# Another order in the attention loop: scaling ahead of the fourth row of logits, exponentials behind the copies, silu one step earlier

## What is computed

```python
for i in range(DEPTH):                                   # DEPTH = 2
    x = x + 0.5 * swiglu(rms_norm(x, ffn1_norm[i]), ...)  # width 2816
    x = x + hybrid_mixer(rms_norm(x, mix_norm[i]), ...)
    x = x + 0.5 * swiglu(rms_norm(x, ffn2_norm[i]), ...)
    gate = sigmoid(rms_norm(x, ple_norm[i]) @ ple_w_gate[i])
    x = x + gate * rms_norm(p[i] @ ple_w_proj[i], ple_post_norm[i])
```

```python
s = einsum('bqhmd,bkhmd->bhmqk', qblk, k) * scale + bias
p = softmax(where(dist >= 0, s, NEG))
o_h = rms_norm(o_h, hgrn_out_norm) * silu(hg)
mixed = concatenate([o_nsa, o_d, o_h]); return mixed @ w_out
```

## Time and profile before

| | us |
|---|---|
| median of 3 runs | 2317.85 |
| lowest, highest | 2317.26, 2318.3 |
| profiled execution | 2319.65 |
| its span | 2317.8 |
| TensorE busy in the span | 2247.7 |
| VectorE, ScalarE, GpSimd busy | 1191.1, 899.1, 155.7 |

### The profile page before, as it was taken

How to read it: one execution, slowest core, us unless ns; L and a number is a source line. 1 busy time by engine, 2 the same in 40 slices (tenths; PEclk the granted TensorE clock), 3 DMA queues, 4 the chain that set the end, 5 groups by cost and what they waited for, 6 DMA issues and landing times. The chain is left out here.

```text
span 2317.8 us, 28783 instructions
## 1 busy us (share of the span) xinstructions
PE 2247.7 (97%) x11400; PEld 1777.9 (77%) x11400; DVE 1191.1 (51%) x1965; ACT 899.1 (39%) x1479; POOL 155.7 (7%) x155
## 2 busy tenths in 40 slices
PE   8999999998989999999999999999989999999998
PEld 6888887776657888888778888877766578888887
DVE  5444434575676444433664443345666754444336
ACT  5222223544664323223552232234556543222334
POOL 0000000043112000000000000001331110000000
PEclk9999999999999999999999999999999899999999
DMA  5333334322103233333223333343120123333332
GB/s 190 129 95 99 93 100 145 103 65 66 52 21 90 93 100 92 97 108 98 90 92 100 97 93 98 95 144 106 55 80 28 29 84 100 100 101 97 97 99 81
DMA packets 68991, 214.38 MB, mean 92 GB/s; under 512 B 8143, under 2 KB 15311, under 8 KB 68858
## 3 DMA queue, kind: packets, MB, share of 16 engines
q1 hardware_dynamic: 59344, 189.27, 26.5%
q10 hardware_dynamic: 9514, 23.27, 3.0%
HBM read 208.30 MB, written 5.40 MB: 92 GB/s over the span
## 5 line engine op out<-in xcount | busy, mean ns | idle before, releaser
L525 PE MATMUL main<-xh,wh 128*128 128x512 f32 x1896 | 757.0, 399 | 12.2 <-DVE xl L1474 8.0
L526 PE MATMUL main<-xl,wh 128*128 128x512 f32 x1896 | 741.2, 391 | 0.0
L527 PE MATMUL main<-xh,wl 128*128 128x512 f32 x1896 | 740.8, 391 | 0.0
L1467 DVE TENSOR_TENSOR wl<-raw,wh 128x1024 fp32r<-128x1024 f32 (+2 forms) x338 | 407.2, 1205 | 376.8 <-ACT wh L983 375.7
L983 ACT ACTIVATE wh<-raw 128x1024 fp32r<-128x1024 f32 (+3 forms) x372 | 377.8, 1017 | 479.8 <-PE main L527 451.6
L525 PEld LDWEIGHTS main<-xh,wh 128*128 128x128 f32 x1896 | 357.2, 188 | 113.9 <-issue 21.3
L527 PEld LDWEIGHTS main<-xh,wl 128*128 128x128 f32 x1896 | 357.5, 189 | 75.7
L526 PEld LDWEIGHTS main<-xl,wh 128*128 128x128 f32 x1896 | 357.5, 189 | 75.1 <-issue 4.3
L525 PE MATMUL main<-ffh,wh 128*128 128x512 f32 x704 | 273.9, 389 | 0.0
L526 PE MATMUL main<-ffl,wh 128*128 128x512 f32 x704 | 273.9, 389 | 0.0
L527 PE MATMUL main<-ffh,wl 128*128 128x512 f32 x704 | 273.9, 389 | 0.0
(11 more groups left out here) (244 smaller groups left out, 2087.5 us busy)
## 6 DMA issues: line engine op xcount, KB each, us to landing
raw<-in_ffn_gate SPq DMA_DIRECT2D x88, 512.0 KB, 3.6
raw<-in_ffn_up SPq DMA_DIRECT2D x88, 512.0 KB, 3.5
raw<-in_ffn_down SPq DMA_DIRECT2D x64, 448.0 KB, 3.3
raw<-in_w_in_t SPq DMA_DIRECT2D x40, 512.0 KB, 3.6
raw<-in_ffn_down SPq DMA_DIRECT2D x32, 512.0 KB, 3.5
raw<-in_wout SPq DMA_DIRECT2D x24, 384.0 KB, 3.2
w<-in_cmp_w ACTq DMA_DIRECT2D x16, 512.0 KB, 3.9
raw<-in_ple_gate SPq DMA_DIRECT2D x16, 512.0 KB, 3.3
```

The lines of the kernel that those rows point to most:

```text
L525: nc.tensor.matmul(out, lh, rh, start=start, stop=False, **kw)
L526: nc.tensor.matmul(out, lh, rl, start=False, stop=False, **kw)
L527: return nc.tensor.matmul(out, ll, rh, start=False, stop=stop, **kw)
L1467: nc.vector.tensor_tensor(wl[:, c % SLOTS, 0:n], raw[:, c % SLOTS, 0:n], wh[:, c % SLOTS, 0:n], ALU.subtract).then_inc(*tick("weights_lo", ...
```

## The change

Three things, in both layers:

- VectorE does rows one to three of `logits(u)`, then `scale(u-1)`, then row four of `logits(u)`.
- ScalarE does rows one to three of the exponentials of map u, then `head_factor` and `split`, then `turned(u-1)`, then row four of the exponentials. `turned(u-1)` now stands ahead of the silu and of `mixed_hi`, which stood ahead of it.
- The silu of the gates moves from step 5 to step 4, behind the fourth exponentials. The wait for the product of `dq1` stays in step 5, ahead of `mixed_hi`.

```diff
+                def exponentials(u, rows):
+                    for i in rows:
+                        for g in range(2):
+                            act.wait_ge(*done("logits", u, g, i))
+                            k = 8 * (u % 2) + 4 * g + i
+                            pr = probs[u % 2][g][:, row0(i):row0(i + 1)]
+                            nc.scalar.activation(pr, pr, ACT.Exp, bias=sm("nm", k), scale=-1.0,
+                                                 accum_out=sm("sum", k)).then_inc(*tick("probs", u, g, i))
...
                         if u < MAPS:
-                            for i in range(QT):
...
+                            exponentials(u, (0, 1, 2))
                         if u == 0:
                             head_factor(("hgrn", 2), HEAD)
...
                             split(CHUNK[("wout_early", OUT_AT[u][0])] + AHEAD)
-                        if u == 5:
+                        if u:
+                            turned(u - 1, ACT_TURNS[u - 1 < NSA_HEADS])
+                        if u < MAPS:
+                            exponentials(u, (3,))
+                        if u == 4:
 
                             act.wait_ge(*done("scaled", "hg2"))
                             nc.scalar.activation(z[:], z[:], ACT.Silu).then_inc(*tick("out_gate"))
                             at["logs"] = False
                             log_tables()
+                        if u == 5:
                             act.wait_ge(*done("product", (GROUP_OF["B"][-1],)))
                         for k in MIXED_AT.get(u, ()):
                             mixed_hi(k)
-                        if u:
-                            turned(u - 1, ACT_TURNS[u - 1 < NSA_HEADS])
...
-                def logits(u):
+                def logits(u, rows):
...
-                    for i in range(QT):
+                    for i in rows:
...
                         if u < MAPS:
-                            logits(u)
+                            logits(u, (0, 1, 2))
                         if u:
                             scale(u - 1)
+                        if u < MAPS:
+                            logits(u, (3,))
```

## The result

The changed kernel takes 2304.41 us (median of 5 runs, 2301.03 to 2307.67), the kernel before 2317.85 beside it (5 runs, 2314.06 to 2323.47). The ratio is 0.9942, 95% interval 0.9926 to 0.9958: 13.4 us faster, where 21.7 were forecast. 2304.41 lies 0.4 us above the forecast range of 2290 to 2304. The profiled execution took 2301.03 us (span 2299.2) and is the fastest of the five; its span is 18.6 us shorter than the 2317.8 of before, 5 us more than the medians differ.

The account below looks back on a forecast made before the run. TensorE, busy 97%, was taken as the bound, so only its idle and slow-clock stretches could be won: 6.9 + 11.0 + 2.8 + 0.9 = 21.7 us off the median 2317.85 gives 2296.2 us, range 2290 to 2304.

Parts of the forecast that it names:

- Silu part: Silu and two table loads, 4.1 us of work, hidden in ScalarE's idle time in step 4, margin 1 us.
- Rival 4: The drain of the table rule is there in step 4; time 2299.4 us, chance 0.03.
- (a) to (d): Walk from the start of step 5 to that of step 7: 23.2 us, gains of 6.9 and 11.0 us.
- T6: Moment TensorE starts step 6 of its loop, with map 5's transposes; forecast 10.0 us after step 5 starts.
- T7: Moment TensorE starts step 7 of its loop, with map 6's transposes; forecast 23.2 us after step 5 starts.
- (e): Step 7 to 8: the VectorE and ScalarE chain ends at 9.6 us, TensorE's work 9.76; gains 1.4 us per layer.
- (b): From step 5's start: six logits of map 6 take 2.15 us, reciprocal at +8.1, step 6 starts at +10.0.
- (f): Step 1: TensorE's wait of 0.56 us for ScalarE's copy goes; counted 0.45 us per layer, 0.9 in all.
- Rival 1: The clock still falls in steps 5 and 6, as several gaps lie close together; 2298 to 2303 us, chance 0.17.
- Rivals 2 and 3: Reordering moves nothing, only the silu helps, 2307 us, 0.08; or the cross-engine ring outlasts TensorE's step, 2337.6 us, 0.03.
- Rival 2: The reordering moves nothing and only silu's step helps: 10.8 us, time 2307, chance 0.08.
- Rival 5: Fewer gaps in TensorE than walked; 2289 to 2293 us, chance 0.09.

Follow-up runs that it names:

- silu_only: The kernel before with the silu alone moved to step 4, behind map 3's copies; 2304.77 us, ratio 0.9942.
- norms_moved: norm_first, with VectorE's norm of `dq1` in step 6 put behind the copies; 2294.49 us, ratio 0.9897.
- norm_first: The changed kernel with VectorE's norm of `dk1` in step 1 ahead of the two other passes; 2295.67 us, ratio 0.9902.
- pool_half: The changed kernel with GpSimd subtracting only half of chunk hg2's low weights, so the output is not the reference's; one run, 2298.85 us.
- scalar_only: The kernel before with ScalarE's order alone, silu in step 5 and VectorE as before; 2320.95 us, ratio 1.0012.
- orders_only: The changed kernel with the silu back in step 5; 2314.1 us, ratio 0.9991.
- gate_early: norm_first, with the three gate products moved up in step 5 to VectorE's idle time; 2294.49 us, ratio 0.9904.

## Why the prediction was wrong, point by point

- **Silu part: right.** It is 4.1 us, hidden in step 4. The drain of some 1.38 us, which the Trainium skill ("ScalarE: Activation LUTs", section "What ACT_TABLE_LOAD costs") adds to each switch, is not there: ScalarE's first table load starts at 635.86, directly behind the exponentials (635.84), and silu at 637.15, 1.29 us later. Rival 4 is out. The silu's worth was undersold: silu_only brings 13.8 us.
- **Steps 5 and 6, (a) to (d): right to 0.2 us, though not wait by wait.** T6 is at +9.79 for +10.0, T7 at +23.11 for +23.2 in both layers, and the gain of 18.2 us stands for the 17.9 of the sum. The chain over VectorE and ScalarE that was to set T6 and T7 does so. TensorE's waits lie elsewhere: 0.48 us ahead of T6 for the 1.4 counted, because its own work in step 5 is 9.31 us and not step 3's 8.6; then 0.55 us for the 0.7 between the groups, no wait for the two banks of the fourth scores (0.2 and 0.3 counted), none to speak of ahead of T7 (1.1 counted; its own work ends level with the chain there), and in their place one that the walk did not have, for VectorE's copies behind the norm of `dq1`:

```profile
659.11 0.92 PE L817 MATMUL side<-dk,dqt 32*128 32x128 f32 x8 [1.20 <-DVE probsT L1894]
```

That norm takes 1.92 us (0.75 before) and has no term in the walk; it had no effect on T7, as norms_moved shows.
- **(e), T7 to T8: size off.** 10.02 and 10.06 us for 9.76, the gain 2.3 us for 2.8. No wait for `scale` is left at T8. The 0.3 us probably go to scores that wait for copies, which now follow two rows of logits and the early sum; no run tests that. By a like mechanism T8 to T9, "nothing changes", grew by 0.36 and 0.33 us: the scores wait 0.3 us for `add_early` (x_res L1975).
- **Slips in the working, without weight.** ScalarE's last copy in step 3 ends 2.54 us after T3, not 2.44. In (b) 6.1 + 2.15 is 8.25, not 8.1. In (e) 3.1 + 0.7 + 2.15 + 3.77 is 9.72, not 9.6, so hardly 0.04 us and not 0.2 were to spare.
- **(f), step 1: the step that failed.** The forecast was a gain of 0.9 us, the change is a loss of 4.8 in the trace: VectorE's norm of `dk1` takes 2.83 us instead of 0.74, the copies behind it come late, and TensorE waits 2.51 us for them. "VectorE's copies free the next banks as late as before" was not so, and "GpSimd's subtractions follow the same splits of the weights" stopped one question short, namely when the splits come: the split came 1.0 us earlier after T1, and so did GpSimd's subtraction, which landed on VectorE's norm. norm_first, pool_half and scalar_only show it three ways. Of the 8.3 us between forecast and result this is the main part, 5.7 us in the traces: with the norm out of the way the kernel is 22.9 us below before, for the 21.7 forecast.
- **Rival 1, the clock: part of it.** In the profiled execution of after the clock stayed at 1.00 in steps 5 and 6 of both layers, as forecast; in other executions it need not. Of the fourteen stretches T6 to T7 in the seven kernels with the whole change, twelve take 13.3 us at a clock of 1.00 and two take 14.7 and 14.8 at 0.88. And behind the new 2.51 us wait of step 1 the clock fell to 0.90 in the first layer and not in the second. That the medians show 5 us less than the profiles fits with this, and with the stretch at 540 to 570 us; the runs that are not profiled show only a mean clock, 0.991 to 0.993 for after.
- **Rivals 2 and 3: no.** T7 to T8 shows that the order works, and orders_only is not slower than before. Rival 2's time, 2307, is close to the measured one by coincidence: the orders did bring nothing on balance (silu_only 13.8 us, the whole change 13.4), but because step 1 took back what steps 5 to 7 gave. Rival 5, fewer gaps than walked: TensorE's gaps in steps 5 and 6 are fewer, 2.2 us for 3.7, but T7 comes no earlier for it.

## What to carry to other kernels

When an instruction is moved off an engine's queue, follow what then starts earlier, through every engine it releases, and put it on the clock beside what runs there: here ScalarE's split came earlier, GpSimd's subtraction with it, and a 0.74 us pass of VectorE became 2.83 us. Of two orders that wait for each other across engines neither was worth anything alone (1.0006, 1.0012), nor both without the silu (0.9991); behind the silu, and with the clash removed, they were worth 9.1 us. A gap of TensorE of two microseconds costs its length and may cost as much again in clock (4.8 us of gaps at T5 and T6 of the kernel before went with 3.5 us of lost clock in one layer and 8.6 in the other), so the largest gap goes first: one moved silu brought as much as the whole change.

## What the runs showed of the hardware

- VectorE's norm, a pass with two SBUF inputs, does not share with GpSimd's SBUF subtraction: wherever it starts behind one, it ends 0.54 to 0.56 us behind GpSimd's end, 18 times in seven kernels, whatever GpSimd's length (2.36, 1.82 or 1.28 us). The profile shows this as busy time of VectorE and not as a wait, so no list of waits names GpSimd. VectorE's copies out of PSUM do not wait (0.56 us in norms_moved beside GpSimd's running instruction in step 6), nor do its sums with one input in PSUM (`x_res`, L1966 of the kernel before: 0.69 us at 674.02, inside GpSimd's instruction from 673.98 to 675.80).
- The granted clock after a gap of the same length is not always the same: behind 2.51 us in step 1 it was 0.90 in one layer and 1.00 in the other of one execution of the changed kernel, 0.83 and 0.82 in orders_only.
- The kernel before has times between 2313.5 and 2324.3 us over 29 runs in one session, at mean clocks between 0.985 and 0.991, against 2293.6 to 2294.6 for five of six runs of gate_early at 0.994 to 0.995; the sixth took 2302.3 at 0.989. With most of its gaps gone the kernel seems to vary less, but six runs are too few to show it.
